# The end of a MoE decode kernel: last expert's rows gated on leaving PSUM, partial sums shared out over three engines

## The reference

```python
gates = jnp.sum(jax.nn.one_hot(sel_i, N_EXPERTS) * weights[..., None], axis=1)
out = jnp.zeros_like(t)
for e in range(N_EXPERTS):
    u = jax.nn.silu(t @ w_gate[e]) * (t @ w_up[e])
    out = out + gates[:, e:e + 1] * (u @ w_down[e])
y = layer_norm(ALPHA * h + f, ln2_g, ln2_b)      # f is out
```

## Time and profile before

| | |
|---|---|
| three runs | 1028.82, 1029.28 (median), 1029.68 us |
| the profiled execution, its own time | 1029.47 us |
| its span in the profile | 1027.7 us |
| mean granted clock of PE | 0.993 |
| busy: PE, DVE, ACT, POOL | 999.9, 793.4, 478.5, 379.0 us |

### The profile page before, as it was taken

The page is one execution under the profiler, slowest core; times in us unless marked ns, Lnnn a source line. Parts: engine busy times, 40 slices in busy tenths (PEclk is TensorE's granted clock), DMA queues, the critical chain, the costliest instruction groups (busy, mean ns, idle before and its releaser), DMA issues.

```text
span 1027.7 us, 19645 instructions
## 1 busy us (share of the span) xinstructions
PE 999.9 (97%) x7246; PEld 904.1 (88%) x7246; DVE 793.4 (77%) x982; ACT 478.5 (47%) x674; POOL 379.0 (37%) x278
## 2 busy tenths in 40 slices
PE   7999999999999999999999999998999999999995
PEld 7999999999999999999999999986677777777773
DVE  4598889888989985844434498237989898999987
ACT  4232322223232335134442323452788887878765
POOL 3444444444454755344544454320200000000355
PEclk9999999999999999999999999998999999999998
DMA  7432323233232222333235522647999999999475
GB/s 219 120 103 82 102 82 97 86 88 95 85 99 82 82 83 73 101 111 91 82 102 162 186 82 92 257 154 286 398 389 397 391 399 389 399 391 399 155 247 179
DMA packets 147290, 190.55 MB, mean 185 GB/s; under 512 B 6819, under 2 KB 114339, under 8 KB 147228
## 3 DMA queue, kind: packets, MB, share of 16 engines
q1 hardware_dynamic: 140107, 176.74, 49.4%
q0 software_dynamic: 3008, 10.55, 3.2%
q10 hardware_dynamic: 4129, 2.67, 0.9%
HBM read 179.16 MB, written 11.76 MB: 186 GB/s over the span
## 4 chain that ended last, share of the span: by engine, by line
PE 91%; DVE 5%; issue 2%; DMA 2%; ACT 1%; POOL 0%; SPq 0%; DVEq 0%; POOLq 0%; ACTq 0%
PE pr L1079 60%; PE pr L1269 16%; PE work L1269 8%; DMA sb_tok<-in_state_conv_b_dram 1%; PE work L1245 1%; PE work L1161 1%; PE pr L1310 1%; PE pr L1289 1%; DMA hs<-h_rows,ids 0%; PE work L1186 0%; DVE y_a L2015 0%; PE work L1087 0%; PE pr L1234 0%; DVE q_hi L1596 0%; PE pr L1178 0%
## 5 line engine op out<-in xcount | busy, mean ns | idle before, releaser
L595 POOL TENSOR_TENSOR w_lo<-raw,w_hi 128x512 fp32r<-128x512 f32 x208 | 297.2, 1449 | 326.8 <-ACT w_hi L724 326.8
L1079 PE MATMUL pr<-x_hi,w_hi 128*128 128x260 f32 x1264 | 255.2, 283 | 0.0
L1079 PE MATMUL pr<-x_hi,w_lo 128*128 128x260 f32 x1264 | 254.8, 283 | 0.0
L1079 PE MATMUL pr<-x_lo,w_hi 128*128 128x260 f32 x1264 | 254.3, 283 | 0.0
L728 ACT ACTIVATE ev<-pr 128x520 f32<-128x520 f32 x96 | 58.2, 606 | 372.7 <-PE pr L1079 372.7
L1079 PEld LDWEIGHTS pr<-x_hi,w_hi 128*128 128x128 f32 x1264 | 195.0, 189 | 0.3
L1079 PEld LDWEIGHTS pr<-x_hi,w_lo 128*128 128x128 f32 x1264 | 194.9, 188 | 0.0
L1079 PEld LDWEIGHTS pr<-x_lo,w_hi 128*128 128x128 f32 x1264 | 194.3, 188 | 0.0
L1522 DVE SCALAR_TENSOR_TENSOR work<-b_pad,par,work 128x512 f32<-128x512 f32 x224 | 148.1, 742 | 0.0
L724 ACT ACTIVATE w_hi<-raw 128x512 fp32r<-128x512 f32 x208 | 118.9, 622 | 3.7 <-DMA raw<-in_w_in_dram 3.4
L632 POOL DMA_INDIRECT hs<-h_rows,ids x15 | 19.3, 1288 | 247.5 <-DVE ids L1801 247.5
(11 more groups left out here) (397 smaller groups left out, 1749.7 us busy)
## 6 DMA issues: line engine op xcount, KB each, us to landing
raw<-in_w_in_dram SPq DMA_DIRECT2D x80, 512.0 KB, 3.7
w_gate<-in_expert_w_gate_dram SPq DMA_DIRECT2D x16, 2048.0 KB, 14.4
w_up<-in_expert_w_up_dram SPq DMA_DIRECT2D x16, 2048.0 KB, 13.0
w_down<-in_expert_w_down_dram SPq DMA_DIRECT2D x16, 2048.0 KB, 12.5
y_rows<-y_out SPq DMA_DIRECT2D x14, 384.0 KB
raw<-in_w_a_out_dram SPq DMA_DIRECT2D x8, 512.0 KB, 4.1
raw<-in_w_c_out_dram SPq DMA_DIRECT2D x8, 512.0 KB, 4.1
raw<-in_w_b_out_dram SPq DMA_DIRECT2D x8, 512.0 KB, 3.9
```

Source lines behind the costliest of these rows:

```text
L595: pool.tensor_tensor(w_lo[:, slot, k], raw[:, slot, k], w_hi[:, slot, k].bitcast(F32), ALU.subtract).then_inc(w_split, 1)
L1079: mm = pe.matmul(pr[slot][:, h, 0:HALF], w[:, slot, k, :], x[:, k, h * HALF:(h + 1) * HALF], start=(k == 0 and w is w_hi and x is hi), sto ...
```

## The change

The last expert's rows are multiplied by each token's weight when they leave PSUM. For that DVE writes the weight of the last expert, in three bf16 parts, beside the token numbers (`weigh_last`), `find_ids` of the last expert brings the parts to the slots, and ACT sums them into `last_gate` (`last_gate_in`). The share is then the plain marks (`share`, zeros and ones), so that `share_lo` and one matmul of three fall away. Its marks, transposes and copy move ahead of the second half of `up_last`, and with them the arithmetic of `slot_ready`. ACT copies each half to `y_last_hi`, waits for DVE's `y_last_lo` (`share_low`) and then copies it to `y_last`.

Partial sums 0 and 1 are made by ACT (a scaling, `weigh_lower`) and POOL (a sum with `h_back`). Partials 2 and 3 stay on DVE and stand earlier in its order. DVE adds the upper row of block 0 to its partial (`others_first`), and PE's product of block 0 goes alone into PSUM. POOL gathers the upper rows of blocks 0 and 1 before its sums, those of 2 and 3 and both sample gathers behind them. The one-element square root moves behind the branch over the further passes. Two constants lie elsewhere in memory. The rest of the diff renumbers semaphore counts.

```diff
+        s_wa, s_wb = s_max, s_sum
...
+        last_cols = sb("last_cols", [P, NTB, 5], BF16)
+        last_gate, gate_parts = sb("last_gate", [C, 1]), sb("gate_parts", [C, 3])
...
             pool.wait_ge(first.done["down"], (E - 1) * CH)
             fetch(y_a, slot_early, y_a_in, y_rows[0:EARLY * C, :])
-            pool.wait_ge(end_dve, 2)
+            pool.wait_ge(slots_ready, 4)
+            pool.wait_ge(first.stored, 16 * E)
+            fetch(y_b, slot_ready, y_b_in, y_rows[0:(E - 1) * C, :], (0, 1))
+            pool.wait_ge(back_in, 48)
+            for b in range(2):
+                pool.wait_ge(end_act, 2 + b)
+                pool.tensor_tensor(plain(y_a[:, b, :]), plain(y_a[:, b, :]), paired(h_back[:, b, :]), ALU.add).then_inc(added, 1)
+            pool.wait_ge(end_dve, 3)
             fetch_samples(sy_a, 0, y_a_in, y_rows[0:EARLY * C, :])
+            fetch(y_b, slot_ready, y_b_in, y_rows[0:(E - 1) * C, :], (2, 3))
...
             with pool.Else():
-                pool.wait_ge(slots_ready, 4)
-                pool.wait_ge(first.stored, 16 * E)
-                fetch(y_b, slot_ready, y_b_in, y_rows[0:(E - 1) * C, :])
                 pool.wait_ge(first.half_stored, 32)
                 fetch_samples(sy_b, 2, y_b_in, y_rows[0:E * C, :])
...
+            def last_gate_in(ps, t):
+                act.wait_ge(ps.ids_ready, t + 2)
+                act.activation(gate_parts[:], pr[1][0:C, 1, 2:5], ACT.Copy, accum_out=last_gate[:]).then_inc(ps.half_ready, 1)
+            def weigh_lower(b):
+                act.wait_ge(slots_ready, 4)
+                act.wait_ge(y_a_in[b], 16)
+                act.activation(y_a[:, b, :], y_a[:, b, :], ACT.Copy, scale=s_wa[:, b:b + 1]).then_inc(end_act, 1)
             def last_rows_out(ps, t, q, row0):
                 x = E - 1
+                act.wait_ge(ps.half_ready, q * 3 + 1)
                 for h in range(2):
                     cols = slice(h * D // 2, (h + 1) * D // 2)
                     act.wait_ge(ps.done["down"], t * CH + CH + 2 * (h + 1))
-                    act.activation(y_last[:, cols], work[0][0:C, h, :], ACT.Copy).then_inc(ps.half_ready, 1)
                     if ps is first:
-                        if h == 0:
-                            act.wait_ge(end_mm, 2)
-                            act.activation(share_hi[:], pr[1][0:C, 1, :], ACT.Copy).then_inc(end_act, 1)
-                        act.activation(y_last_hi[:, cols], work[0][0:C, h, :], ACT.Copy).then_inc(end_act, 1)
-                    act.wait_ge(ps.half_ready, q * 2 + (h + 1))
+                        act.activation(y_last_hi[:, cols], work[0][0:C, h, :], ACT.Copy, scale=last_gate[:]).then_inc(end_act, 1)
+                        act.wait_ge(end_dve, 4 + h)
+                    act.activation(y_last[:, cols], work[0][0:C, h, :], ACT.Copy, scale=last_gate[:]).then_inc(ps.half_ready, 1)
+                    act.wait_ge(ps.half_ready, q * 3 + (h + 2))
                     act.dma_start(y_rows[bass.ds(x * C + row0, C), cols], y_last[:, cols]).then_inc(ps.half_stored, 16)
...
+                    if m == 13:
+                        last_gate_in(ps, t + 2)
...
                 rounded_parts(ps, "down", 0, uses[0] + 5, t, last=True, chunks=(0, 1))
+                if ps is first:
+                    act.wait_ge(end_mm, 1)
+                    act.activation(share[:], pr[1][0:C, 1, :], ACT.Copy).then_inc(end_act, 1)
                 u_in_last(ps, t, 0)
                 rounded_parts(ps, "down", 0, uses[0] + 5, t, last=True, chunks=(2, 3))
+                if ps is first:
+                    weigh_lower(0)
                 u_in_last(ps, t, 1)
+                if ps is first:
+                    weigh_lower(1)
                 last_rows_out(ps, t, q, row0)
...
-            act.activation(r_tok[0:1, 0:1], eps_t[0:1, 0:1], ACT.Sqrt)
             n_max = further_passes(act)
...
             with act.Else():
                 act.nop()
+            act.activation(r_tok[0:1, 0:1], eps_t[0:1, 0:1], ACT.Sqrt)
             normalised()
...
                         up_last(ps, t, 0, x_hi_t, x_lo_t)
+                        if ps is first:
+                            pe.wait_ge(end_dve, 1)
+                            for b in range(4):
+                                mm = pe.transpose(pr[1][0:C, 1, b * P:(b + 1) * P], share_tok[:, b, :], ident[:])
+                            mm.then_inc(end_mm, 1)
                         pe.wait_ge(ps.silu_ready, t + 2)
...
                     pe.wait_ge(const_ready, 6)
-                    pe.wait_ge(end_dve, 1)
+                    pe.wait_ge(end_dve, 2)
+                    pe.wait_ge(end_act, 1)
                     pe.matmul(pr[1][:, 1, 8:13], spread[:], s_own[:], start=True, stop=True).then_inc(end_mm, 1)
                 down_last(ps, t, 0, 0)
                 turn_u_part(ps, t, 1)
                 down_last(ps, t, 1, 0)
                 down_last(ps, t, 0, 1)
-                if ps is first:
-                    pe.wait_ge(end_dve, 3)
-                    for b in range(4):
-                        mm = pe.transpose(pr[1][0:C, 1, b * P:(b + 1) * P], share_tok[:, b, :], ident[:])
-                    mm.then_inc(end_mm, 1)
                 down_last(ps, t, 1, 1)
                 if ps is first:
                     share_last()
             def share_last():
-                def part(b, h):
+                def others(b):
+                    for h in range(2):
+                        pe.matmul(z_tile[b][:, h, :], ident[:], y_a[:, b, h * D // 2:(h + 1) * D // 2], start=True, stop=False)
+                def own(b, h):
                     n = slice(b * P, (b + 1) * P)
                     cols = slice(h * D // 2, (h + 1) * D // 2)
-                    pe.matmul(z_tile[b][:, h, :], ident[:], y_a[:, b, cols], start=True, stop=False)
-                    for w, y in ((share_hi, y_last_hi), (share_lo, y_last_hi), (share_hi, y_last_lo)):
-                        mm = pe.matmul(z_tile[b][:, h, :], w[:, n], y[:, cols], start=False, stop=y is y_last_lo)
+                    for y in (y_last_hi, y_last_lo):
+                        mm = pe.matmul(z_tile[b][:, h, :], share[:, n], y[:, cols], start=b == 0 and y is y_last_hi, stop=y is y_last_lo)
                     return mm
-                pe.wait_ge(end_dve, 5)
-                pe.wait_ge(partial_ready, 1)
-                part(0, 0)
-                pe.wait_ge(end_dve, 6)
-                part(0, 1).then_inc(end_mm, 1)
-                for b in (1, 2, 3):
-                    pe.wait_ge(partial_ready, b + 1)
-                    part(b, 0)
-                    part(b, 1).then_inc(end_mm, 1)
+                pe.wait_ge(added, 2)
+                others(1)
+                for h in range(2):
+                    pe.wait_ge(end_act, 4 + h)
+                    pe.wait_ge(end_dve, 4 + h)
+                    mm = own(0, h)
+                mm.then_inc(end_mm, 1)
+                own(1, 0)
+                own(1, 1).then_inc(end_mm, 1)
+                for b in (2, 3):
+                    pe.wait_ge(partial_ready, b - 1)
+                    if b == 3:
+                        pe.wait_ge(first.half_ready, 3)
+                    others(b)
+                    own(b, 0)
+                    own(b, 1).then_inc(end_mm, 1)
...
+            def weigh_last():
+                x = TURN[E - 1]
+                own = lambda t: t[:, :, x:x + 1].rearrange("p b o -> p (b o)")
+                part = lambda j: last_cols[:, :, j:j + 1].rearrange("p b o -> p (b o)")
+                do(dve.tensor_tensor(s_t[:], own(oh1), s_w1[:], ALU.mult))
+                do(dve.tensor_copy(last_cols[:, :, 0:2], id_cols[:]))
+                step(dve.tensor_tensor(s_max[:], own(oh2), s_w2[:], ALU.mult))
+                step(dve.tensor_tensor(s_t[:], s_t[:], s_max[:], ALU.add))
+                for j in (2, 3):
+                    step(dve.tensor_copy(part(j), s_t[:]))
+                    step(dve.tensor_tensor(s_t[:], s_t[:], part(j), ALU.subtract))
+                do(dve.tensor_copy(part(4), s_t[:]), Tally(dve, bias_ready, 2))
+                last[0] = chain
...
                         low_parts(ps, "up", s, t, slots="down")
+                        if ps is first:
+                            share_marks()
+                            ready_slots()
...
                 gated_part(ps, t, 1)
+                if ps is first:
+                    dve.wait_ge(back_in, 48)
+                    partial(2, 16)
                 low_parts(ps, "down", 0, t, (2,), last=True)
                 u_low_last(ps, t, 1)
+                if ps is first:
+                    spread_samples()
                 low_parts(ps, "down", 0, t, (3,), last=True)
                 if ps is first:
-                    spread_samples()
-                    share_marks()
-                    partials(16)
-            s_wa, s_wb = s_max, s_sum
+                    partial(3, 16)
+                    share_low(0)
+                    others_first()
+                    share_low(1)
```

(36 more changed lines are left out.)

81 lines of the change are left out of this document (34 added, 47 removed).

## The result

The change makes the kernel slower. Six runs of each, in turns: 1028.95 us before (median, 1027.73 to 1029.68), 1034.38 us after (1032.64 to 1035.33); ratio 1.0053, 95% interval 1.0042 to 1.0063. So 5.4 us were lost. The profiled execution after took 1032.64 us, the fastest of its six, with a span of 1030.9 us. Five more runs of the same kernel gave 1035.01 us (ratio 1.0058), profiled at 1035.01.

A forecast was written before the change was run, and what follows sets the result against it. The end is bound by DVE's first normalisation, ACT's squares having 1.27 us in hand. Late squares put it 2.9 us later, POOL's collision 3.5 more: 6.4, so 1029.47 + 6.4 - 0.19 = 1035.7 us, range 1029.0 to 1038.5.

The forecast's parts named there:

- The early parts at nothing: `weigh_last`, `last_gate_in`, `share_marks` and `ready_slots` hide in existing waits; 0 to 2 us if `weigh_last`'s cover were gone.
- PE's transposes, 0.4: Four transposes moved ahead of the second half of `up_last` delay the halves of u by 0.3 to 0.6 us.
- The partial of block 2 waits for its gather to 997.2: DVE, there at 995.4, waits for y_a's gather, so down's last low part ends at 1001.3 against 998.46.
- The hand-over, L + 5.4: ACT and DVE alternate on each half; last store 5.4 us after L, the end of `low_parts` 3, against 4.2 before.
- POOL and DVE, +3.5: POOL's two sums collide with DVE's two-SBUF-input operations around 997 to 1003; 2.7 to 4.3 us, taken as 3.5.
- The 4.86 us behind the store move with it: ACT's time from last store to table load stays 4.86 us; 1.6 might be saved if the old dummy root held the branch.
- The range: 1029.0 to 1038.5 us; the upper end counts both POOL sums in full (+7.6) and 1.6 for strided operands.
- B: Rival: block 2's gather of y_a is there in time; 1030.4 us, or 1029 with 1.6 saved at the branch; chance 0.12.
- A: Rival: no contention that matters, POOL's sums fall into DVE's waits; 1032.2 us; chance 0.15.
- D: Rival: PE's clock falls after idling ahead of the last halves, a dozen matmuls double; +2 us, 1037.7; chance 0.05.
- C: Rival: the branch does not come behind the last store, so DVE decides; faster, 1027.6 to 1026.3 us; chance 0.15.
- Of what would show it: Profile signs: DVE's gather wait, stretched low parts or POOL sum above 3, store near 1010, normalisation near 1017.7 released by ACT.

The follow-up runs named there:

- e1_order: Changed kernel, with DVE making the low part of the last expert's second half before `others_first` instead of behind it: 1031.17 us, ratio 1.0025.
- e4_sums_early: Changed kernel, with POOL's two sums ahead of its gathers of y_b for blocks 0 and 1: 1036.14 us, ratio 1.0066.
- e5_root_alone: Kernel before, with only ACT's dummy square root moved behind the branch over the further passes: 1028.88 us, ratio 1.0000.
- e2: Changed kernel, with ACT copying each half for the store first, no longer waiting for DVE's low part: 1031.48 us, ratio 1.0023.
- e7: Changed kernel, with the second half's low part ahead of `others_first` and ACT's copy for the store ahead of the high part: 1031.69 us, ratio 1.0026.
- e10_dve_copy_order: Changed kernel, with all four weighted sums on DVE, the copy for the store first, the second half's low part ahead of `others_first`: 1028.21 us, ratio 0.9988.
- e8_own_first: Changed kernel, with low part and store copy moved ahead, and PE forming the last expert's share of block 0 before block 1: 1030.25 us, ratio 1.0013.
- e6_dve_partials: Changed kernel, with ACT's scalings and POOL's sums undone, DVE forming all four weighted sums: 1031.84 us, ratio 1.0026.

## Why the prediction was right, and where it was not

Direction and cause held: slower, since ACT's last store is late, the branch, table load and squares follow it, and POOL's sums collide with DVE. 6.4 us were forecast, 5.4 measured (6.4 in the second set of runs). Two of its steps were wrong in place or size, the wait for the gather and the collision. They made the forecast 3.1 us too high at the first normalisation, and two terms that were too low, the hand-over and the stretch, gave 1.5 of it back; that the number came so near is in part luck.

*The early parts at nothing*: they fit. `weigh_last` is nine operations, not eleven; DVE's wait for ACT behind it is 3.05 us instead of 4.92. The first low part of down starts 2.64 us behind the copy of the fifteenth expert in the kernel before and 2.60 in the changed one; the marks and the ten small operations fill the hole of 1.73 us.

*PE's transposes, 0.4*: `gated_part` 1 comes 0.15 us later in both profiles.

*The partial of block 2 waits for its gather to 997.2*: wrong. It ran at 993.90 without a wait. The gather of 990.54 goes out at 982.16 in the changed kernel. The step took the gathers' issue for fixed. In the row of 6.95 us, POOL only waits: it ends 0.82 us behind the last of DVE's back-to-back operations, as the prediction says itself two parts later, and in the changed kernel the gather issued at 983.62, beside the same series of DVE, took only 1.96 us. What decides how long one is held, no run shows. So the end of low part 3 moved from 9.96 to 10.77, +0.8 and not +2.8.

*The hand-over, L + 5.4*: without POOL in the way 5.95 (e1_order: 998.48 to 1004.43). Right as a mechanism, 0.55 short.

*POOL and DVE, +3.5*: the place was wrong and the size nearly right, the latter in part by luck, since it was worked out for a place where the two did not meet. Not the low parts but `others_first` paid, 0.93 us of waiting and 2.13 of its 3.40. On the way to the last store that comes to 2.4 us: from L to the store it is 8.36 us in the changed kernel (998.03 to 1006.39) and 5.95 where the low part goes ahead. POOL's sums stand behind gathers that wait for the fifteenth's store, which the prediction overlooked when it let them start at 997.1. Put where it had them (e4_sums_early), they hold DVE for 1.8 and 2.2 us, 4.0 in all, within its 2.7 to 4.3; what that alone would do to the time is not shown, as the gathers were late there too. The Trainium skill says that a VectorE instruction with two SBUF inputs contends with a GpSimd instruction that reads SBUF (SBUF — State Buffer, "Who interferes with whom"); the trace agrees, with 3.40 us against 1.27.

*The 4.86 us behind the store move with it*: they follow, but they are no constant. They are 3.60 to 6.31 us over these kernels. With the gathers alone held back they were 3.87 instead of 5.83. The moved root had little part in it: 5.12 us against 4.86 (e5_root_alone).

The terms, put right, give the trace: 6.4, less 2.0 for the gather, less 1.1 for the collision, plus 0.55 for the hand-over, plus 0.97 for the stretch, are 4.8; the first normalisation is 4.84 late. The sum closes because its terms are read from this trace, with e1_order used only to part the hand-over from the collision. In the second profile it is 6.23 late, with a last store 0.9 later and a stretch 0.5 longer still.

*The range.* Its upper end counts 1.6 us for strided operands, for which no run has a row: POOL's sums took 2.45 us each, against 2.37 in the earlier trace rows.

*The rivals.* B's premise, the gather in time, was true, but not its result, as it left the collision out. A is refuted by the row of 3.40. D was right that the clock falls, and wrong on where: not ahead of the last halves but in the 3.48 us before the combine. In the changed kernel it costs nothing, as ACT is later still (DVE has its two sums at 1012.6, ACT's squares at 1014.8); with ACT out of the way, PE with its wait for POOL and its halved clock is the bound (e1, e2, e7). C needed ACT out of the way, DVE's and PE's waits for POOL gone, and short stretches at the branch: e10_dve_copy_order has the first two, and its 0.12% are less than the 0.2% that the prediction called measurable. That kernel keeps the early parts, the share of plain marks and the constants in their new place, so these cost nothing that its time shows.

*Of what would show it*: the wait for the gather did not appear, the stretched low parts neither; POOL's sums took 2.45 each. The late store (19.1, foreseen near 21.5) and DVE idle for ACT's squares (2.21 and 3.79 us in the two profiles, foreseen some 4) did. The start of the normalisation, foreseen near 1017.7, which is 29.2 in position, was 27.65 and 29.04.

What stays open: in e4_sums_early the stretch is the shortest of all, 3.60 us, although gathers still fill the queues when it begins; they thin out some 1.5 us into it, and queue 14's packet comes at 1013.5 to 1014.0. Between the store and the packet there are 142 packets of the gathers, as many as the kernel before has (145) with a stretch of 4.86 us. So the number of packets alone does not settle it. This was not tried apart, and neither was a version in which the gathers go out early enough to be over before the branch.

## What to carry to other kernels

An engine that helps is free only if nobody who matters is queued behind the place where the two meet. Here two sums taken off DVE (2.5 us) cost it 3.1 us at one addition, and made PE idle into half its clock; before moving work to GpSimd, look at what VectorE's queue holds at that moment, and at what the helper's own queue makes it wait for. And when a store or copy is gated on another engine, read on from it to the next branch: everything behind moves with it.

## What was not expected of the hardware

From ACT's last store to its first instruction behind the branch over code that isn't run, 3.6 to 6.3 us go by here, and the figure goes with what the DMA queues carry: 3.87 with the gathers held back, 5.83 and 6.31 with them. On DVE no more than 1.16 us go by at it (e8_own_first).

A GpSimd sum and a VectorE operation of two SBUF inputs don't share but queue: the VectorE operation of 1024 columns ends 1.08 to 1.10 us behind GpSimd's pair in eight kernels, and even an operation of three columns is held, 1.93 us for 0.16.

After 3.4 to 4.5 us without a matmul the granted clock of TensorE was 0.50, 1.2 GHz, and the matmuls that followed took up to twice as long (3.47 to 3.78 against 1.88 us for four); after 1.89 us (e6_dve_partials) it was still 1.00. In e8_own_first idle stretches of 0.89, 0.63 and 1.54 us with a few matmuls between them were followed by 0.52.
